# Sparse attention of a two-block network run step by step beside its projection, compression and output product

## What is computed

```
q, kc, vc, ks, vs, kw, vw, gates = split(h @ w_in)    # 16 q heads, 4 kv heads of 64; w_in: 1024 x 2608
q  = rmsnorm(q, q_norm)
kc = rmsnorm(compress_blocks(kc, pos[0], w1[0], w2[0]), k_norm[0])   # blocks of 32 tokens, stride 16: 15 of them
vc = compress_blocks(vc, pos[1], w1[1], w2[1])        # gelu((blocks + pos) @ w1) @ w2
ks = rmsnorm(ks, k_norm[1]);  kw = rmsnorm(kw, k_norm[2])
o_cmp = attention(q, kc, vc); o_sel = attention(q, ks, vs); o_win = attention(q, kw, vw)
g = sigmoid(gates)
y = (g0 * o_cmp + g1 * o_sel + g2 * o_win) @ w_out
```

## Time and profile before

| | before |
|---|---|
| median of 3 runs (lowest, highest) | 1375.97 us (1373.01, 1379.57) |
| the profiled execution | 1373.45 us, span 1371.6 us |
| mean granted TensorE clock | 0.975 of 2.4 GHz |
| PE busy, PE weight load busy | 1287.5 us (94%), 1201.2 us (88%) |
| DVE, ACT, POOL busy | 861.8 us (63%), 575.3 us (42%), 222.2 us (16%) |
| HBM | 172 GB/s over the span |

### The profile page before, as it was taken

One profiled execution on the slowest core, in us unless ns is written; L12 is line 12 of the kernel. 1 busy time (PEld: TensorE's weight loads), 2 busy tenths in 40 slices (PEclk: granted clock), 3 DMA queues, 4 the chain that ended last, 5 costly groups with the idle time before them and its releaser, 6 DMA issues.

```text
span 1371.6 us, 21647 instructions
## 1 busy us (share of the span) xinstructions
PE 1287.5 (94%) x9040; PEld 1201.2 (88%) x9040; DVE 861.8 (63%) x865; ACT 575.3 (42%) x690; POOL 222.2 (16%) x233
## 2 busy tenths in 40 slices
PE   2888889989999999998999999999999998899998
PEld 2887789879999999886899999899999996899997
DVE  5679675665555657887655555655556776655554
ACT  1332444343333355774433333433334666433331
POOL 4095139068200010000100000100001121200000
PEclk9999989999999999799999999999999999999999
DMA  9596566445555454400465555455554543355551
GB/s 361 187 313 231 192 215 208 161 128 191 188 188 190 157 185 137 146 1 18 154 197 184 183 183 184 155 187 185 188 188 144 178 156 113 118 191 187 187 187 62
DMA packets 166819, 236.93 MB, mean 173 GB/s; under 512 B 5141, under 2 KB 146593, under 8 KB 164705
## 3 DMA queue, kind: packets, MB, share of 16 engines
q1 hardware_dynamic: 165920, 235.09, 51.4%
q0 software_dynamic: 816, 0.89, 0.2%
q10 hardware_dynamic: 16, 0.00, 0.0%
HBM read 234.92 MB, written 1.05 MB: 172 GB/s over the span
## 4 chain that ended last, share of the span: by engine, by line
PE 74%; DVE 14%; DMA 5%; ACT 4%; issue 1%; POOL 1%; DVEq 0%; ACTq 0%; POOLq 0%
PE acc L1677 13%; PE acc L1679 13%; PE acc L1678 13%; PE acc L1712 6%; PE acc L1713 6%; PE acc L1714 6%; DVE wlo L1028 3%; DMA raw<-in_w_in_dram 2%; PE acc L1695 2%; PE acc L1697 2%; PE acc L1696 2%; DVE region L1035 2%; PE acc L1738 2%; PE acc L1737 2%; PE acc L1736 2%; ACT whi L649 2%
## 5 line engine op out<-in xcount | busy, mean ns | idle before, releaser
L1028 DVE TENSOR_TENSOR wlo<-raw,whi 128x2048 fp32r<-128x2048 f32 x199 | 463.5, 2330 | 312.8 <-ACT whi L649 311.5
L1677 PE MATMUL acc<-hT_hi,whi 128*128 128x256 f32 x1792 | 514.8, 287 | 25.9 <-DVE wlo L1028 12.9
L649 ACT ACTIVATE whi<-raw 128x2048 fp32r<-128x2048 f32 x199 | 379.1, 1905 | 365.0 <-PE acc L1714 151.4
L1678 PE MATMUL acc<-hT_lo,whi 128*128 128x256 f32 x1792 | 511.5, 285 | 0.0
L1679 PE MATMUL acc<-hT_hi,wlo 128*128 128x256 f32 x1792 | 511.3, 285 | 0.0
L1677 PEld LDWEIGHTS acc<-hT_hi,whi 128*128 128x128 f32 x1792 | 348.3, 194 | 31.5 <-DVE wlo L1028 15.6
L1678 PEld LDWEIGHTS acc<-hT_lo,whi 128*128 128x128 f32 x1792 | 348.6, 195 | 1.7 <-issue 0.2
L1679 PEld LDWEIGHTS acc<-hT_hi,wlo 128*128 128x128 f32 x1792 | 348.4, 194 | 0.0
L1712 PE MATMUL acc<-whi,sT_hi 128*128 128x512 f32 x336 | 132.3, 394 | 4.5 <-ACT bias L766 4.1
L1713 PE MATMUL acc<-wlo,sT_hi 128*128 128x512 f32 x336 | 131.9, 393 | 0.0
L1714 PE MATMUL acc<-whi,sT_lo 128*128 128x512 f32 x336 | 131.2, 390 | 0.0
(11 more groups left out here) (272 smaller groups left out, 1419.3 us busy)
## 6 DMA issues: line engine op xcount, KB each, us to landing
raw<-in_ffn_w_in_dram SPq DMA_DIRECT2D x88, 1024.0 KB, 5.1
raw<-in_ffn_w_out_dram SPq DMA_DIRECT2D x44, 1024.0 KB, 5.0
raw<-in_w_ada_dram SPq DMA_DIRECT2D x24, 1024.0 KB, 5.3
raw<-in_w_in_dram SPq DMA_DIRECT2D x24, 1024.0 KB, 5.4
raw<-in_diff_w_in_dram SPq DMA_DIRECT2D x12, 1024.0 KB, 5.2
raw<-in_nsa_w_in_dram SPq DMA_DIRECT2D x10, 1024.0 KB, 5.4
raw<-in_w_out_dram SPq DMA_DIRECT2D x8, 1024.0 KB, 5.0
raw<-in_nsa_cmp_w_dram SPq DMA_DIRECT2D x4, 1024.0 KB, 6.2
```

Of the source, the lines that this page charges most:

```text
L649: nc.scalar.activation(whi[:, w % SPL, 0:n], raw[:, r % RAW, 0:n], ACT.Copy).then_inc(hi_ready, 1)
L1028: nc.vector.tensor_tensor(wlo[:, w % SPL, 0:n], raw[:, r % RAW, 0:n], whi_f[:, w % SPL, 0:n], ALU.subtract).then_inc(raw_done, 1)
L1677: nc.tensor.matmul(o, hi[:, kt, cs], hT_hi[:, kt, :], start=kt == 0, stop=False)
L1678: nc.tensor.matmul(o, hi[:, kt, cs], hT_lo[:, kt, :], start=False, stop=False)
```

## The change

The change rewrites the NSA stage's order on PE, ACT, DVE and POOL; nothing else of the program moves. Its parts:

- The projection goes through banks 0 and 1 alone, in the order keys, gates, values, q of head group 0, 1, kc, q 2, vc, then q 3 after the first two compression chunks. A chunk is run in two halves (128 tokens each, `token_half`).
- The 20 steps are reordered: for each of three kv heads sel, win; then cmp 0, sel 3, cmp 1, win 3. Each is put by hand between half chunks, compression chunks or quarters of output chunks. All steps share one pair of score banks (2 and 3), and steps 0 to 15 share one value bank (7). So scores(p) waits for the maximum of p-1, and values(p) for the combine of p-1.
- Norms: for the keys and for each q group ACT squares, DVE reduces, POOL computes (mean + eps) ^ -0.5 in two instructions, DVE scales; DVE's own `rsqrt` goes. The compressed keys' norm goes to POOL as well.
- kc and vc are transposed once (8 transposes instead of 16) and DVE builds the blocks out of PSUM in four calls of ten instructions; before it was eight instructions in all, and four copies by DVE and four by ACT.
- A combine multiplies with one instruction over 256 columns instead of two over 128.
- ACT switches between exponential and gelu twice instead of once.

```diff
-NSA_ORDER = [4, 5, 0, 1, 2, 3, 6, 8, 7, 9, 10]
+NSA_ORDER = [6, 8, 0, 10, 7, 1, 9, 4, 2, 5, 3]
...
+            def inverse_heads(n, at):
+
+                w = at.stop - at.start
+                pool.wait_ge(sq_free, n)
+                step(nc.gpsimd.tensor_scalar(ms[:, 0:w], stat[:, at], 1.0 / DH, EPS, ALU.mult, ALU.add))
+                nc.gpsimd.tensor_tensor(rs[:, at], ms[:, 0:w], power[:, 0:w], ALU.pow).then_inc(qrs_ready, 1)
...
-        nsa_steps = [(b, hkv, tt) for b in ("sel", "win") for hkv in range(HKV) for tt in range(TT)]
-        nsa_steps += [("cmp", half, tt) for half in range(2) for tt in range(TT)]
+        nsa_steps = [(b, hkv, tt) for hkv in range(3) for b in ("sel", "win") for tt in range(TT)]
+        nsa_steps += [(b, at, tt) for b, at in (("cmp", 0), ("sel", 3), ("cmp", 1), ("win", 3)) for tt in range(TT)]
...
+        def pv_bank(p):
+
+            return 7 if p < 16 else 2 if p == 19 else 1
...
+            n0 = w_at[("nsa", NSA_ORDER[0])]
+            for i in range(10):
...
+                if i == 6:
+                    reduce_q(1)
+                    nsa_max(2)
+                    evict_nsa_k(1)
...
+                stream_to(n0 + i + LEAD)
...
+                if i == 5:
+                    nsa_max(1)
+                if i == 6:
+                    scale_q(1)
+                    nsa_max(3)
+                    combine(0)
...
+            def nsa_scores(p):
...
+                if p:
+                    pe.wait_ge(scored, p)
...
+            def nsa_values(p):
...
+                pe.wait_ge(pT_act, p + 1)
+                if p:
+                    pe.wait_ge(combined, p)
...
+            for i in range(10):
+                nsa_half(i, 0)
...
+                if i == 5:
+                    nsa_scores(1)
+                    turn_k(1)
+                if i == 6:
+                    nsa_turn(1)
+                    nsa_values(0)
+                    nsa_scores(3)
...
+                nsa_half(i, 1)
...
+                if i == 5:
+                    nsa_turn(0)
+                    nsa_scores(2)
+                if i == 6:
+                    nsa_turn(2)
+                    nsa_values(1)
+                    turn_q(1)
```

More of the change, by code:

```diff
@@ L112, in stream_items @@
     items += ffn(0)
-    items += [("w", "nsa", c) for c in NSA_ORDER]
-    items += [("w", "cmp", kv, half) for kv in range(2) for half in range(2)]
+    items += [("w", "nsa", c) for c in NSA_ORDER[:10]]
+    items += [("w", "cmp", 0, half) for half in range(2)]
+    items += [("w", "nsa", NSA_ORDER[10])]
+    items += [("w", "cmp", 1, half) for half in range(2)]
     items += [("w", "nsao", c) for c in range(4)]
@@ L779, in ffn_all @@
                 ffn(q)
[L781 to L809, removed]
@@ new lines, in cmp_chunk @@
+            def cmp_chunk(kv, half):
+                w = w_at[("cmp", kv, half)]
+                chunk_ready(w)
+                if half == 0:
+                    pe.wait_ge(cmpr_ready, 2 * kv + 2)
+                    if kv == 0:
+                        pe.wait_ge(proj_ready, 24 + 9)
+                    else:
+                        pe.wait_ge(gelu_ready, 1)
+                hi = whi[:, w % SPL, :].rearrange("p (k n) -> p k n", k=8)
+                lo = wlo[:, w % SPL, :].rearrange("p (k n) -> p k n", k=8)
+                o = acc[:, 0, 0:CMP_HIDDEN]
+                for k in range(8):
+                    m = 8 * half + k
+                    c0 = (CMP_TILES * (1 - kv) + m) * rows
+                    bh, bl = (v[:, c0:c0 + P] for v in cmp_flat)
+                    nc.tensor.matmul(o, bh, hi[:, k, :], start=m == 0, stop=False)
+                    nc.tensor.matmul(o, bh, lo[:, k, :], start=False, stop=False)
+                    ins = nc.tensor.matmul(o, bl, hi[:, k, :], start=False, stop=m == 15)
+                ins.then_inc(chunk_used, 1)
@@ new lines, in turn_to, with turn_k @@
+            def turn_to(bank, at, src):
+                return nc.tensor.transpose(acc[:, bank, at:at + P], src, ident[:, :])
+            def turn_k(h):
+                pe.wait_ge(kn_ready, h + 1)
+                if h in (1, 2):
+                    pe.wait_ge(qk_act, h)
+                if h == 3:
+                    pe.wait_ge(cmpr_ready, 2)
+                for b in range(2):
+                    for tt in range(TT):
+                        ins = turn_to(4, b * T + tt * P, key_twice(h)[:, tt, b, :])
+                ins.then_inc(k_turned, 1)
@@ new lines, in turn_q @@
+            def turn_q(h):
+                pe.wait_ge(qn_ready, h + 1)
+                if h < 2:
+                    pe.wait_ge(qk_dve, h + 1)
+                elif h == 2:
+                    pe.wait_ge(qk_dve, 4)
+                else:
+                    pe.wait_ge(cmp_sb, 2)
+                for pair in range(2):
+                    for tt in range(TT):
+                        ins = turn_to(4, pair * T + tt * P, pj[:, tt, (2 * h + pair) * P:(2 * h + pair + 1) * P])
+                ins.then_inc(q_turned, 1)
@@ L1875, in scores @@
                     e, slot = m % 2, m // 2
[L1876 to L1886 removed]
+                    half = slice(e * DH, (e + 1) * DH)
@@ new lines, in _ @@
+            pe.wait_ge(kcn_ready, 2)
+            nc.tensor.transpose(acc[:, 4, 384:384 + rows], kcn.rearrange("p c d -> p (c d)"), ident[0:rows, 0:rows])\
+              .then_inc(kcn_ps, 1)
+            cmp_chunk(1, 1)
+            nsa_turn(11)
+            nsa_values(10)
+            turn_q(3)
+            nsa_scores(12)
+            nsa_scores(13)
+            turn_gelu(1)
+            nsa_values(11)
+            nsa_turn(12)
+            nsa_scores(14)
+            cmp_layer2(1)
+            nsa_turn(13)
```

985 lines of the change are left out of this document (605 added, 380 removed).

## The result

| | before | after |
|---|---|---|
| median (lowest, highest) | 1375.97 us (1373.01, 1379.57) | 1409.67 us (1407.16, 1411.67) |
| ratio, 95% interval | | 1.0248 (1.0212 to 1.0285) |
| the profiled execution, span | 1373.45 us, 1371.6 us | 1407.16 us, 1405.4 us |
| mean granted clock | 0.975 | 0.966 |
| NSA stage, first projection to last output matmul | 188.8 us | 222.1 us |

The account below looks back on a forecast made before the run. PE, busy 94% of the program, was taken as the bound. Queue walk +15.3, late results -2, POOL's norms +2.5 and clock +3 made +18.8 on 1373.45, so 1392 us; range 1370 to 1406.

Parts of the forecast that it names:

- The walk: NSA stage's four queues followed instruction by instruction, PE at 2.4 GHz: work 159, waits 45, 204 us against 188.8, +15.3.
- Scores(2): In chunk 5, PE waits 3.3 us for DVE's maximum of step 1, since scores share one pair of banks.
- Values(1): In chunk 6, PE waits 4.7 us for DVE's combine of step 0, since values share bank 7.
- the compressed keys' norm: In the first half of compression chunk 1, PE waits 3.7 us for this norm.
- steps 13 to 17: Hardly any chunk stands there; values(13), values(15) and the output's transposes each wait for a combine, 10.1 us of waits.
- the term of +3 us: Half clock in the new stage, added to the full-clock walk: 3 us, bounds 0 to 14.
- the tail's 6: Half-clock cost if the whole new stage ran at the DIFF stage tail's clock of 0.96: 6 us.
- the bound of 14: Upper bound of the half-clock term, if the new stage's clock were 0.91: 14 us.
- half clock through the middle: Rival: gaps of 2 to 5 us bring the stage's clock to 0.83, +23 in place of 3, 1412 us; 7%.
- The last sign of being wrong: In the profile after, a stage long only because the clock is below 0.9.
- POOL's norms: POOL's first small instruction waits out a DVE split at q 0 and q 3: +0.7 and +1.8, together +2.5 us.
- a split waits behind each power: Rival: DVE's next instruction waits for POOL's power at all five norms, 8 us in place of 2.5, 1398 us; 5%.

Follow-up runs that it names:

- f2_hold: The changed kernel with b1's four moves, gate chunk at 256 columns, unread matmuls in remaining waits and 30 more among short products; 1386.5 us.
- b1: The changed kernel with four queue moves: maximum 1, combine 0 and combine 4 earlier on DVE, copy of step 18 earlier on ACT; 1399.3 us, ratio 1.0165.
- c2: The kernel before with the gate chunk at 256 columns and 66 unread 256-column matmuls around its attention's start and end; 1365.1 us, ratio 0.9924.
- b2_dve_q: The changed kernel with the four q groups' inverse roots moved back from POOL to DVE; 1422.9 us, ratio 1.0335.
- e4_moves: The changed kernel with eleven queue moves, b1's four among them, no unread matmuls and a gate chunk of 48 columns; 1402.3 us, ratio 1.0182.
- a1: The changed kernel with the gate chunk's 48 matmuls reading 256 columns instead of 48; 1413.5 us, ratio 1.0256.
- c1: The kernel before with the gate chunk's 48 matmuls reading 256 columns instead of 48; 1377.6 us, ratio 1.0006.
- e2: c2 with its 66 unread matmuls 48 columns wide in place of 256; 1372.7 us, ratio 0.9968.

## Why the prediction failed

**The sum at full clock** was about right, as far as the runs show. The walk had 204 us, less 2 for results taken late. The changed kernel itself never ran at full clock. f2_hold did, in 200.2 us, but with four moves that took 7.6 us of waits out in b1; with these put back, my estimate for the changed kernel is 200 to 208. In the sum as measured, two terms were off against each other. PE's work is 165 us, not 159: in c2, at full clock, 172.5 less 66 x 0.12 = 164.6; in f2 188.7 less 188 x 0.12 = 166. The waits are 34, not 43, at half clock in places.

**The waits** were at their places. Scores(2): 3.3 forecast, 3.16 measured. Values(1): 4.7, 3.58. Chunk 8, kc's transpose in it: 2.4, 2.5 (1.95 and 0.56). Values(5) 3.2, 1.81. Scores(10) 2.3, 2.12. Gelu 3.0, 3.08. Values(18) 3.7, 2.94. Two were much shorter: the compressed keys' norm, 3.7 for 1.58, and steps 13 to 17, 10.1 for 5.8 (PE's idle time from 626 to 656 us). The second lies in the longest stretch at half clock, where PE comes late to each wait.

**The clock is the step that failed**: the term of +3 us. "I take 3, between nothing and the tail's 6, since most of the stage is full chunks". Against 165 us of work, PE's busy 188.0 us hold 23 us of half clock; before they held 13. So the term measured 23, not 3, and the bound of 14 was too low as well. Two faults led there. I took the clock from one stretch of the DIFF stage with the same idle share (0.96), as if the share decided; but that stretch has no 48-column chunk, no 20 us of short products and no wait above 1.66 us, where the changed stage has four of 2.9 to 3.6. And the walk set 34 us of half clock of the kernel before to zero before it added 3 for the new mixture. The rival that I gave 7%, half clock through the middle, 1412 us at 0.83 (the median is 1409.7 at 0.86), is what happened: not in an even mixture, but in pieces, in and behind the gate chunk, behind each of these four waits (0.50 over 676 to 680 us behind the last), and from 626 to 648 us, where steps 12 to 15 have no chunk beside them. Its size was near too: a net +23 there, and 222.1 us against the 200 to 208 above is 14 to 22 more. The last sign of being wrong that I gave, a stage long only by a clock below 0.9, came half true: the clock was 0.86, and the waits were there as well.

From the forecast's 207.6 us of the stage to 222.1: work +6, clock +20, waits -9, POOL -2.5. Clock and waits aren't independent, since the half clock itself shortened the waits; that the errors of work and waits nearly cancel is luck.

**POOL's norms**: +2.5 was too much; b2_dve_q shows that they gain. At q 0 the small instruction went as forecast:

```profile
500.33 2.17 POOL L584 TENSOR_SCALAR ms<-stat 128x8 f32<-128x8 f32 x1 [3.49 <-DVE stat L1526]
...
617.64 0.20 POOL L584 TENSOR_SCALAR ms<-stat 128x8 f32<-128x8 f32 x1 [1.26 <-DVE stat L1526]
```

```profile
500.16 2.28 DVE L1154 TENSOR_TENSOR wlo<-raw,whi 128x2048 fp32r<-128x2048 f32 x1
504.27 0.69 DVE L1535 TENSOR_TENSOR proj<-proj,rs 128x512 f32<-128x512 f32 x1 [1.83 <-POOL rs L585]
```

The 0.20 us instruction took 2.17 and ended with the split, as in the earlier trace rows, and DVE waited 1.83 us; PE did not feel it. At q 3 ACT's part of the split was late, POOL was through in 0.20, and nothing was lost. The Trainium skill (SBUF — State Buffer, Who interferes with whom) has a DVE instruction with two SBUF inputs contend with a GpSimd one that reads SBUF, by an exclusive lock; the small one at q 0 agrees, but the 16-column power of the keys again ran its 2.94 us beside a split of 2.29. So the rival "a split waits behind each power" is out here.

**Table loads**: five, as forecast, 1.28 us each. The next instruction starts 1.29 us behind the load's start, so no drain is seen behind it:

```profile
600.43 1.28 ACT L906 ACT_TABLE_LOAD   x1
601.72 0.38 ACT L906 ACTIVATE lam<-acc 60x256 f32<-60x256 f32 x1
```

**The range** left the half clock out by choice ("leaves out the faster case and the half clock"), with 7% for it. With the clock of 0.83 seen in the attention before, the only row with such products, it should have been the likelier value of an unmeasured term. The range was also narrower than its own bounds: from 1392.3, a clock term of 14 in place of 3 and waits wrong by 6 reach 1383 to 1409, not 1381 to 1406, and the new median was allowed 2.5 more. That range would have ended at 1412 and held the 1409.7, without the clock term being any better.

## What to carry to other kernels

A walk of the queues at full clock finds the waits; price the clock as a term of its own, from rows with the same operand widths, and start it from what the kernel before already loses. Work woven in "beside" other work gained nothing here, where each step passes one bank between three queues that also carry whole splits; no run gave the steps a second bank, so what the shared bank alone costs stays open. Before moving a step, name who waits for the instruction that it is moved in front of: b1_order kept most of what it removed, in e4_moves it came back at the next user. Half clock cost nothing where another engine was late behind it (a1, c1); where PE is the chain, 66 wide matmuls of no use around its small gaps and short products bought 10 us.

## What was not expected of the hardware

- In a chunk of 48 products of 48 columns, PE busy without a gap, the clock falls to half (0.72 over 495.9 to 508 us); the same 48 at 256 columns keep 1.00 and take 0.12 us each for 0.11.
- `keep` matmuls of 256 columns held the clock at 1.00 for the whole stage (c2, f2, both with the wide gate chunk), as many of 48 columns didn't (0.57 over 571 to 591 us in e2). Short products without any gap ran at 1.00 for 30 us (590 to 620, before).
- In the set with c1 and c2, the kernel before took 1366.3 to 1368.7 us in 3 of 17 executions, at a mean clock of 0.980 to 0.984, and 1375.4 to 1379.5 in the others, at 0.969 to 0.975. c2 stays within 1363.5 to 1369.1, at 0.985 to 0.991: its gain is about what the kernel before has in its fastest executions, of which no profile was kept; that their dips are shorter is my guess from the mean clock.
